# Two edits at the end of a decoder step: when the gate half of a channel tile is computed, and in which order the down projection is fed

## The reference, cut to what matters

```
def conv_ffn(x, s_conv, norm_w, w_up, conv_w, conv_b, w_down):
    h = rmsnorm(x, norm_w)
    gt, up = split_cols(h @ w_up, (D_FF, D_FF))
    gt, new_conv = causal_dwconv(gt, s_conv, conv_w)
    return x + (jax.nn.silu(gt + conv_b) * up) @ w_down, new_conv
...
    y = rmsnorm(x, norm_f_w)
```

## Time and profile before

| | |
|---|---|
| median of 3 runs | 2953.02 us |
| the profiled execution | 2951.56 us |
| its span | 2949.8 us |
| TensorE busy (matmul) | 2749.9 us, 93% |
| TensorE weight load | 2610.4 us, 88% |
| VectorE | 1900.1 us, 64% |
| ScalarE | 1316.1 us, 45% |
| GpSimd (POOL) | 878.8 us, 30% |
| granted TensorE clock, mean | 0.963 |
| chain that ended last: down products (L2728) | 7% of the span |

### The profile page before, as it was taken

The page is one execution under the profiler, slowest core; times in us unless marked ns, Lnnn a source line. Parts: engine busy times, 40 slices in busy tenths (PEclk is TensorE's granted clock), DMA queues, the critical chain, the costliest instruction groups (busy, mean ns, idle before and its releaser), DMA issues. The chain is left out here.

```text
span 2949.8 us, 55279 instructions
## 1 busy us (share of the span) xinstructions
PE 2749.9 (93%) x20770; PEld 2610.4 (88%) x20770; DVE 1900.1 (64%) x3172; ACT 1316.1 (45%) x2598; POOL 878.8 (30%) x812
## 2 busy tenths in 40 slices
PE   5999999999999899999998869999989999987998
PEld 5999999999999788878886439999989999987998
DVE  7788888734443588888887554554386666653453
ACT  5545555444444355555554243342344444433432
POOL 2555555512332332433233210000233333320100
PEclk8999999999999999999998769999989999998999
DMA  3233333422343333443336367654522122226543
GB/s 101 91 107 100 109 113 104 137 98 92 111 136 130 84 71 81 96 97 79 71 71 134 125 218 248 218 164 138 187 82 83 71 84 103 81 85 251 190 149 107
DMA packets 270209, 353.63 MB, mean 120 GB/s; under 512 B 157672, under 2 KB 186792, under 8 KB 269840
## 3 DMA queue, kind: packets, MB, share of 16 engines
q1 hardware_dynamic: 264976, 330.64, 35.6%
q0 software_dynamic: 4992, 19.74, 1.9%
HBM read 252.96 MB, written 97.38 MB: 119 GB/s over the span
## 5 line engine op out<-in xcount | busy, mean ns | idle before, releaser
L487 PE MATMUL pps<-h_hi,pwh 128*128 128x272 f32 (+1 forms) x2464 | 709.1, 288 | 21.8 <-DVE h_lo L731 10.3
L487 PE MATMUL pps<-h_lo,pwh 128*128 128x272 f32 (+1 forms) x2464 | 708.5, 288 | 0.0
L487 PE MATMUL pps<-h_hi,pwl 128*128 128x272 f32 (+1 forms) x2464 | 706.3, 287 | 0.0
L487 PEld LDWEIGHTS pps<-h_hi,pwh 128*128 128x128 f32 x2464 | 468.3, 190 | 23.7 <-DVE pwl L741 9.7
L487 PEld LDWEIGHTS pps<-h_hi,pwl 128*128 128x128 f32 x2464 | 466.9, 190 | 0.0
L487 PEld LDWEIGHTS pps<-h_lo,pwh 128*128 128x128 f32 x2464 | 466.8, 189 | 0.1
L741 DVE TENSOR_TENSOR pwl<-pw,pwh 128x512 fp32r<-128x512 f32 x176 | 182.9, 1041 | 161.4 <-ACT pwh L553 160.9
L3390 PE MATMUL u_ps<-m_flat,u_wh 128*128 128x266 f32 x1232 | 237.2, 288 | 8.7 <-DVE m_flat L3561 8.7
L2728 PE MATMUL merge_ps<-merge_yh,merge_wh 128*128 128x352 f32 (+1 forms) x576 | 188.5, 327 | 22.0 <-DVE merge_wl L2720 21.0
L783 DVE SCALAR_TENSOR_TENSOR merge_raw<-merge_raw 128x1096 f32<-128x1096 f32 x144 | 204.7, 1421 | 0.0
L2728 PE MATMUL down_ps<-down_yh,down_wh 128*128 128x352 f32 (+1 forms) x528 | 174.4, 330 | 31.3 <-DVE down_wl L2720 29.8
(11 more groups left out here) (491 smaller groups left out, 6802.2 us busy)
## 6 DMA issues: line engine op xcount, KB each, us to landing
projected<-pO SPq DMA_DIRECT2D x88, 536.0 KB, 3.0
pw<-in_w_in SPq DMA_DIRECT2D x176, 256.0 KB, 2.9
merge_w<-in_w_out SPq DMA_DIRECT2D x72, 512.0 KB, 3.6
down_w<-in_w_down SPq DMA_DIRECT2D x48, 704.0 KB, 4.1
u_w<-in_w_up SPq DMA_DIRECT2D x88, 256.0 KB, 2.6
scan_chunk<-projected SPq DMA_DIRECT2D x5, 2496.0 KB, 11.7
ffn<-u_V SPq DMA_DIRECT2D x22, 530.0 KB, 2.9
merge_raw<-projected SPq DMA_DIRECT2D x4, 2496.0 KB, 11.3
```

What stands on the lines that cost most here:

```text
L487: ins = pe.matmul(out, l[s % RING][:, k, :], r[b][:, j, k, :], start=(begins and k == 0 and a == 0), stop=(k == HK - 1 and a == 2), skip_g ...
```

## The change

It has two parts.

In the up projection the two tiles of a pair change places in `w_up`: the up half is now u = 0 and the gate u = 1. The gate's rows are thus complete with join 3, at j = 6 of the same pair, and V is first written by join 1 and last by join 4. The waits go with them: join 1 (now at j = 4) waits for the store of the pair before, join 2 no longer. First tap, second and third tap, silu and gating stand at j = 6, 0, 1, 1 and 2, where they stood at 0, 1, 2, 2 and 3 of the next pair.

In the down projection `HEAD` = 5 of the 11 tiles of the first weight unit (320 KB) are loaded during the up projection, into free columns behind `raw`, and split from there; the other six (384 KB) are loaded at the phase's start. The activations are converted and waited for in three parts of 3, 2 and 6 tiles. The residual of a pass is loaded at the start of the pass (before: all three at the phase's start), the norm's weights at that of pass 1. The first two output tiles of pass 0 are written out in front of the loop.

```diff
@@ down_phase
-        y_hi, y_lo = Event(nc, "down_y_hi", 2), Event(nc, "down_y_lo", 2)
-        halves = (range(ku // 2 + 1), range(ku // 2 + 1, ku))
+        y_hi, y_lo = Event(nc, "down_y_hi", 3), Event(nc, "down_y_lo", 3)
+        parts = (range(HEAD // 2 + 1), range(HEAD // 2 + 1, HEAD), range(HEAD, ku))
...
         @block.sync
-            for s in range(2 * nu):
-                if s == 1:
+            def load_x(n):
+                c0, cn = NTAIL[n]
+                sp.dma_start(x[:, :, c0:c0 + cn], x2[:, :, c0:c0 + cn]).then_inc(x_in.sems[n], 16)
+            def start(n):
+                if n:
+                    load_x(n)
+                if n == 1:
+                    sp.dma_start(w[:, :], d["norm_f"]).then_inc(w_in.sems[0], 16)
+            sp.dma_start(ring.raw[:, 0, HEAD:ku, :], d["w_down"][0, :, HEAD:ku, :]).then_inc(ring.loaded.sems[0], 16)
+            for s in range(1, 2 * nu):
+                if s == 2:
                     sp.wait_ge(ring.loaded.sems[0], ring.loaded.at(0))
                 ring.load(sp, s, s, s)
-            for n, (c0, cn) in enumerate(NTAIL):
-                sp.dma_start(x[:, :, c0:c0 + cn], x2[:, :, c0:c0 + cn]).then_inc(x_in.sems[n], 16)
-            sp.dma_start(w[:, :], d["norm_f"]).then_inc(w_in.sems[0], 16)
+            load_x(0)
...
         @block.tensor
+            pe.wait_ge(head_lo.sem, head_lo.at(0))
...
+                    ahead = isinstance(s0, int) and s0 + unit == 0
+                    if not ahead:
+                        pe.wait_ge(ring.lo_done.sem, ring.lo_done.at(s0 + unit))
+                    for part, ks in enumerate(parts):
+                        pe.wait_ge(y_lo.sem, y_lo.at(nu * n + unit, part + 1))
+                        if ahead and ks[0] == HEAD:
+                            pe.wait_ge(ring.lo_done.sem, ring.lo_done.at(0))
...
         @block.scalar
+            def split_rest():
+                act.wait_ge(ring.loaded.sems[0], ring.loaded.at(0))
+                act.activation(ring.hi[0][:, HEAD:ku, :], ring.raw[:, 0, HEAD:ku, :], ACT.Copy).then_inc(ring.hi_done.sem, 1)
             def start(n):
+                if n == 0:
+                    act.activation(ring.hi[0][:, 0:HEAD, :], head, ACT.Copy).then_inc(head_hi.sem, 1)
+                    convert(0, 0, split_rest)
+                    convert(0, 1, lambda: ring.split_hi(act, 1, 1, 1, 1))
@@ feed_phase, SP, pair 13
+                    sp.dma_start(head, d["w_down"][0, :, 0:HEAD, :]).then_inc(first_in.sems[0], 16)
@@ feed_phase, ScalarE
-                act.wait_ge(joined[1].sem, joined[1].at(p, 4))
+                act.wait_ge(joined[1].sem, joined[1].at(p, 3))
...
-                if p and j == 0:
-                    tap_first(p - 1)
-                if p and j == 2:
+                if j == 6:
+                    tap_first(p)
+                if p and j == 1:
                     finish(p - 1)
@@ feed_phase, VectorE, join
                 if k == 1:
-                    if p >= 2:
-                        dve.wait_ge(new_got.sem, new_got.at(p - 2))
+                    if p:
+                        dve.wait_ge(stored.sems[0], stored.at(p - 1))
...
                 if k == 2:
-                    if p:
-                        dve.wait_ge(stored.sems[0], stored.at(p - 1))
+                    if p >= 2:
+                        dve.wait_ge(new_got.sem, new_got.at(p - 2))
...
-                if u:
+                if u == 0:
                     ins = dve.tensor_tensor(V[:, cols], s, q, ALU.add)
@@ feed_phase, VectorE, regular
-                if p and j in (1, 2):
-                    next_tap(p - 1, j)
-                if p and j == 3:
+                if p and j in (0, 1):
+                    next_tap(p - 1, j + 1)
+                if p and j == 2:
                     gate(p - 1)
-                for k, at in ((1, 3), (2, 5), (3, 6)):
+                for k, at in ((1, 4), (2, 5), (3, 6)):
@@ kernel
-        "w_up": weight_tiles(arr(w_up)[0])[np.arange(2 * FT).reshape(2, FT).T.ravel()],
+        "w_up": weight_tiles(arr(w_up)[0])[np.arange(2 * FT).reshape(2, FT)[::-1].T.ravel()],
```

More of the change, by code:

```diff
@@ L2914, in _, with down_phase @@
             steps(dve, start, body)
-def down_phase(nc, d, source, x, x2, ones, raw):
+HEAD = 5
+def down_phase(nc, d, source, x, x2, ones, raw, head):
     CN, ku, nu = CQ, FT // 2, 2
@@ L2948, in steps @@
                 start(n)
-                with eng.Fori(0, pairs - 1) as i:
+                if n == 0:
+                    for u in range(2):
+                        body(0, u, u, 0, u * nu)
+                with eng.Fori(1 if n == 0 else 0, pairs - 1) as i:
                     for u in range(2):
@@ L2981, in norm @@
                     sp.dma_start(d["y"][:, ks, c0:c0 + cn], x[:, ks, c0:c0 + cn]).then_inc(stored.sems[0], 16)
-            steps(sp, lambda n: None, body, norm)
+            steps(sp, start, body, norm)
             sp.wait_ge(stored.sems[0], stored.at(0))
@@ L3022, in body @@
                 for unit in range(nu):
-                    pe.wait_ge(ring.lo_done.sem, ring.lo_done.at(s0 + unit))
-                    for half, ks in enumerate(halves):
-                        pe.wait_ge(y_lo.sem, y_lo.at(nu * n + unit, half + 1))
+                    ahead = isinstance(s0, int) and s0 + unit == 0
[5 more added lines that the diff above has]
+                            pe.wait_ge(ring.lo_done.sem, ring.lo_done.at(0))
                         ins = ring.product(pe, unit, ps[:, u, 0:cn], lambda k: yh[:, unit * ku + k, 0:cn],
@@ L3040, in _, with convert @@
         def _(act):
-            prime(act, y_hi, ring.hi_done, ln_done, rstd_done, *squared)
-            def convert(n, unit, after_first=lambda: None):
+            prime(act, y_hi, head_hi, ring.hi_done, ln_done, rstd_done, *squared)
+            def convert(n, unit, then=lambda: None):
                 cn, k = NTAIL[n][1], unit * ku
@@ L3048, in convert @@
                     act.wait_ge(ring.used.sem, ring.used.at((KD * n - 1) * nu + unit))
-                for half, ks in enumerate(halves):
+                for part, ks in enumerate(parts):
                     act.activation(yh[:, k + ks[0]:k + ks[-1] + 1, 0:cn], raw[:, unit, ks[0]:ks[-1] + 1, 0:cn], ACT.Copy).then_inc(y_hi.sem, 1)
-                    if half == 0:
-                        after_first()
+                    if part == 1:
+                        then()
+            def split_rest():
+                act.wait_ge(ring.loaded.sems[0], ring.loaded.at(0))
+                act.activation(ring.hi[0][:, HEAD:ku, :], ring.raw[:, 0, HEAD:ku, :], ACT.Copy).then_inc(ring.hi_done.sem, 1)
             def start(n):
-                for unit in range(nu if n == 0 else 0):
-                    convert(n, unit, lambda: ring.split_hi(act, unit, unit, unit, 1))
+                if n == 0:
+                    act.activation(ring.hi[0][:, 0:HEAD, :], head, ACT.Copy).then_inc(head_hi.sem, 1)
+                    convert(0, 0, split_rest)
+                    convert(0, 1, lambda: ring.split_hi(act, 1, 1, 1, 1))
                 if n == 0:
@@ L3088, in _, with convert, split_rest @@
         def _(dve):
-            prime(dve, y_lo, ring.lo_done, eps_set, scaled, *read)
+            prime(dve, y_lo, head_lo, ring.lo_done, eps_set, scaled, *read)
             dve.memset(eps[:, :], EPS).then_inc(eps_set.sem, 1)
-            def convert(n, unit, after_first=lambda: None):
+            def convert(n, unit, then=lambda: None):
                 cn, k = NTAIL[n][1], unit * ku
[L3094 to L3100, removed]
-            def start(n):
-                for unit in range(nu if n == 0 else 0):
-                    convert(n, unit, lambda: ring.split_lo(dve, unit, unit, unit))
+                for part, ks in enumerate(parts):
+                    dve.wait_ge(y_hi.sem, y_hi.at(nu * n + unit, part + 1))
+                    at = slice(k + ks[0], k + ks[-1] + 1)
+                    dve.tensor_tensor(yl[:, at, 0:cn], raw[:, unit, ks[0]:ks[-1] + 1, 0:cn],
+                                      yh[:, at, 0:cn].bitcast(F32), ALU.subtract).then_inc(y_lo.sem, 1)
+                    if part == 1:
+                        then()
+            def split_rest():
+                dve.wait_ge(ring.hi_done.sem, ring.hi_done.at(0))
+                dve.tensor_tensor(ring.lo[0][:, HEAD:ku, :], ring.raw[:, 0, HEAD:ku, :], ring.hi[0][:, HEAD:ku, :].bitcast(F32),
+                                  ALU.subtract).then_inc(ring.lo_done.sem, 1)
+            def start(n):
+                if n == 0:
+                    dve.wait_ge(head_hi.sem, head_hi.at(0))
+                    dve.tensor_tensor(ring.lo[0][:, 0:HEAD, :], head, ring.hi[0][:, 0:HEAD, :].bitcast(F32),
+                                      ALU.subtract).then_inc(head_lo.sem, 1)
+                    convert(0, 0, split_rest)
+                    convert(0, 1, lambda: ring.split_lo(dve, 1, 1, 1))
             def body(n, m, u, rnd, s0):
@@ L3127, in _, with feed_phase @@
```

(12 more changed lines are left out.)

7 lines of the change are left out of this document (4 added, 3 removed).

## The result

The changed kernel ("after" below) takes 2964.65 us (median of 6 runs, 2962.79 to 2970.05) where the kernel before took 2953.2 on the same chips (6 runs, 2946.53 to 2955.6): ratio 1.0044, 95% interval 1.0033 to 1.0056. Forecast were 2945 us, range 2934 to 2953. The profiled execution of after is the slowest of its runs (2970.05, span 2968.3).

The account below looks back on a forecast made before the run. The prediction took TensorE, busy 421.20 of 421.20 us, to bound the up projection, with two idle holes (20.00 and 9.83 us) around the down projection's start; 2951.6 - 17.6 (down) + 11.2 (up) = 2945.2, put at 2945 us, range 2934 to 2953.

Parts of the forecast that it names:

- Up projection, 20 times: Up loop: join 1 waits for the previous tile's store, holding A22 0.56 us in tiles 1 to 20, 11.2 us lost.
- the store is the new bound: Second rival, up loop: store lands in 4.4 us or more, A22 held 1.4 us a tile, 28 us, 2962; chance 0.06.
- 3.55: Up loop: us taken for the store's landing behind the fourth load, giving A22 a wait of 0.56 us.
- The other estimate: Up loop: the skill page's fit put the store's landing at 3.45 us from issue, wait 0.46 us, term 9 us.
- 0 (2.9 us) and 18 (3.9 us): Up loop: bounds of the total loss in us, with the store landing assumed for each in brackets.
- Second hole: Down projection, wait for the fifth weight unit: 9.83 us idle and 2.6 us at lower clock go, 12.4 us gained.
- Hand-over and first units: Start of the down projection: earlier entry and earlier first two weight units, 5.2 us gained (4 to 7).
- The hand-over alone: Up to down projection: last tile's taps start one step earlier, every engine enters the down phase 2.7 us sooner.
- the third rival: Down projection: residual and POOL's loads delay the fifth unit 5 us, 7.6 of 12.4 us lost, 2953; chance 0.10.
- Store issued 17.1 us after A22: Up loop, SP's queue: the store is issued some 0.4 us behind the next tile's fourth-quarter load.
- A wait of VectorE for `ffn<-u_V` in each tile, ended holes before A22: Signs, up loop: VectorE waits about 1 us a tile; TensorE holes of about half a microsecond, ended by DVE `u_V`.
- The head's load: Up loop, tile 13: 320 KB behind a store and ahead of a 1936 KB load cost at most 1 us once.

Follow-up runs that it names:

- e2: Before with only the up projection's part of the change (gate tile second), the down projection as before: 2982.3 us, ratio 1.0097 to before.
- e10: After with the store of V issued by GpSimd in its own queue instead of by SP: 2966.6 us, ratio 1.0039 to before.
- e9: After with two buffers for V and VectorE's second join ahead of the sixth unit's weight split: 2931.3 us, ratio 0.9921 to before.
- e6: Before with only the residual loaded pass by pass (and the norm's weights at pass 1): 2942.0 us, ratio 0.9963 to before.
- e3: After with the previous tile's store issued ahead of the fourth weight load instead of behind it: 2936.4 us, ratio 0.9945 to before.
- e1: Before with only the down projection's part of the change (residual by pass, head, three parts): 2938.5 us, ratio 0.9945 to before.

## Why the prediction was wrong

**Wrong: the landing of the store, in "Up projection, 20 times".** The mechanism was the one written down: join 1 into V, store behind the fourth load, A22 held, 20 times. The size failed: 11.2 us were put for the term, 31 came by the medians (e2's 28.5 and the 3.0 that its hand-over gave back), 34.3 by (a). The rival "the store is the new bound", with a chance of 0.06, put 28 us, and that this is near is partly luck: its landing of 4.4 us or more wasn't reached (4.2), its reason (one queue, one after the other) is refuted by e10, and some 10 of the 34 us come from two things that it didn't have, S4's wait and two tiles with late stores. The store closes a ring, and the period is its sum: A22 to the next store's issue, landing, landing to A22. Forecast: 17.12 + 3.55 + 0.47 = 21.14 us. Measured on the tile above, from its predecessor's A22 at 2608.55: 17.34 + 4.18 + 0.57 = 22.09. So 0.63 of the 0.95 us missed is the landing; 0.22 is S4, which waits for join 2 behind a split that takes 1.5 us (the wait of 0.20 stands in the ring: A22, S4, next store); 0.10 is the way from landing to TensorE. The prediction had join 2 at nothing because it "is where it was"; e9 shows the price, for these waits go when it is moved. 20 x 1.5 = 30, and two tiles lost 3.3 and 2.4 more; (a) has 34.3 and not 35.7, since some tiles lost less.

Where did 3.55 come from? The only row with one load ahead of a store had 3.9; I went 0.35 below it because its load was slower than the ones of the loop. But in after this load is slower too, 3.2 us for 2.6. Two things are new around it, the third load, issued 2.3 us earlier and not yet landed, and the store 0.4 us behind it; which of them slows it the runs don't separate. Either way the discount took for given what the change itself makes worse. The next 23 stores of the input projection have three loads each in the 2.2 us ahead of them and land in 4.3 to 6.0 us; they were there to be read. One of them, with its last two loads (issues from 107.5 to 108.5 in before):
```profile
projected<-pO SPq DMA_DIRECT2D x1, 536.0 KB, 5.6
pw<-in_w_in SPq DMA_DIRECT2D x2, 256.0 KB, 4.6
```
No load ahead 3.0, one 3.9, three 5.1 (medians, but for the one): as an estimate 0.7 to 0.9 us for each load, and none of these stores with loads ahead is near 3.55. The other estimate, by the Trainium skill's fit in "DMA: Bandwidth & Descriptors" ("Anatomy of one DMA — SWDGE (gpsimd) path"), was 3.45 us from the store's issue; the trace disagrees by 0.7.

Also wrong were the bounds: "0 (2.9 us) and 18 (3.9 us)" ended at the one row, with nothing for a landing above it, though the term is 20 times the error.

**Right: the down projection.** Second hole: 12.4 forecast, 11.7 by e6's medians, 13.7 in its trace. Hand-over and first units: 5.2 forecast, 19.8 - 13.7 = 6.1 left for them in (b). The hand-over alone: 2.7 forecast; last store's issue 4.6 us behind the last up product's start for 7.4 before, 2.8. In all 17.6 forecast, 19.8 found. The fifth unit's weights land at 2704.45, before they are due, and the third rival did not occur.

**Right about the queue's timing.** Store issued 17.1 us after A22 forecast (17.34), 0.4 us behind the load (0.37). A wait of VectorE for `ffn<-u_V` in each tile, ended holes before A22: both seen, at twice the size. The head's load was put at "at most 1 us once", and it cost less: A22 of tile 13 waited 1.41 us (1.1 to 1.2 elsewhere), and 1.62 in e2, which has the 1936 KB load there but no head. The 2.4 us above were lost one tile earlier, before either was issued (2494.4 and 2494.8; more on them in the last section).

**Carried over as a margin that wasn't one.** The forecast's own numbers had A22 due at 2429.16 and the store's chain done at 2429.1 at best. A step that costs nothing only at the most favourable end of its price, in a loop of 20, on the engine that is never idle, should have had its range from that end upwards, past the one row at hand.

## What to carry to other kernels

When a change moves the first write of a single-buffered row earlier, write the ring down (who frees it, who issues, who lands, who writes) and compare its length with the loop's period; every 0.1 us is multiplied by the number of rounds, so price a shared DMA by the worst like row of the trace. Then look at what stands ahead of the store: issuing it before the neighbouring load, or giving the row a second buffer, gave back nearly all of the loss here, while another queue gave nothing. And take a double change apart: the good half (-0.55%) was hidden behind the bad one (+0.97%).

## What the runs showed of the hardware

- The same 530 KB store lands in 2.9 us with the nearest load 1.25 us ahead of it (before), in 3.7 with one 1.2 us ahead and one 1.0 behind (e3), in 4.2 with one 0.4 ahead (after), and in 4.2 when it goes out by another queue 0.3 us behind the load (e10). By that queue and with no load near it took 3.1.
- Waits of 1.1 to 1.4 us on TensorE left its clock at 1.00; behind one of 2.3 us (until 2475.20 of after) it was 0.53 for 2.8 us, and behind one of 3.2 it fell as well. After, behind that one, which ended at 2296.59 (columns as in the first fence):
```profile
2296.60:2300.00 3.40, 3.38 (x20) 3.40 (x21) 1.65 (x5) 1.22 (x3) 0.89 (x2) 0.69 0.11 19
2300.00:2304.00 4.00, 4.00 (x30) 4.00 (x30) 1.71 (x4) 1.25 (x2) 0.32 (x2) 0.84 0.13 49
2304.00:2312.00 8.00, 8.00 (x68) 8.00 (x67) 4.41 (x6) 4.33 (x8) 2.27 (x1) 1.00 0.01 2
```
  Between the two levels, 1.2 and 2.4 GHz (0.50 and 1.00), these windows are mixtures: 20 and 30 products where 28 and 33 would fit.
- That tile's store landed in 6.2 us, and in 6.1 and 5.2 us in the same tile of e2 and e3; the store of tile 12 in 5.3, and in 5.7 in e2. In each of these five flights the traces have one 16 KB transfer of the instruction queue (q8), starting 1.4 to 3.1 us behind the store's issue, and in the loop of after in no other store's. The DMA view of after from 2289.7 to 2296.1, 0.16 us a column:
```profile
GB/s 0 0 0 0 141 64 90 115 154 256 307 283 420 409 409 398 410 410 398 473 106 53 27 0 0 26 0 0 26 0 26 26 26 26 26 26 0 0 0 0
...
q8 instruction: 1, 0.02, 1.0%
```
  The last 2 us run at 26 GB/s, a sixteenth of the 410 before: it looks as if one of the 16 engines were late alone. In the loops of all runs nine stores landed in 4.9 us or more; eight have such a transfer in flight, the ninth (e10) the 1936 KB load 0.3 us behind it. But others with one landed as usual (e1: 2.9 to 3.3 us three times, 4.8 once). No run changes these transfers, so the two are seen together, and the cause isn't shown.
